# Final combine of a mixture-of-experts block: idle TensorE products ahead of the weighted sums, and one gather moved up Pool's list

## What is computed

```python
e_w, e_idx = lax.top_k(e_prob, MOE_TOP_K)            # two experts per token
w = g_w * e_w / sum(e_w)
out = einsum('tef,efd->td', silu(gate) * up * combine, w_down)   # = w0*y0 + w1*y1 per token
x = x + g2 * rms_norm(out, post_norm_ffn[l])
```

## Time and profile before

| what | us |
|---|---|
| median of 3 runs | 970.72 |
| lowest and highest run | 970.71, 973.47 |
| the profiled execution, its own time | 972.9 |
| its span, first to last instruction | 971.1 |

### The profile page before, as it was taken

One profiled execution on the slowest core, in us unless ns is written; L12 is line 12 of the kernel. 1 busy time (PEld: TensorE's weight loads), 2 busy tenths in 40 slices (PEclk: granted clock), 3 DMA queues, 4 the chain that ended last, 5 costly groups with the idle time before them and its releaser, 6 DMA issues.

```text
span 971.1 us, 15126 instructions
## 1 busy us (share of the span) xinstructions
PE 923.7 (95%) x5341; PEld 544.2 (56%) x5341; DVE 518.7 (53%) x959; ACT 318.5 (33%) x649; POOL 232.9 (24%) x282
## 2 busy tenths in 40 slices
PE   8999999999989999998999999989999999999953
PEld 6544444444546666667656665575555555555521
DVE  3375447444765666666588885663333333333347
ACT  3230002212545434432233332243333333333333
POOL 2200001122700670002354422012222222222125
PEclk9999999999999999999999999999999999999977
DMA  9996425000490000006023327978999999999694
GB/s 340 385 329 230 181 100 142 0 1 0 171 410 32 2 1 1 2 1 241 23 87 117 101 87 309 411 243 318 401 423 374 423 412 404 416 418 411 243 355 194
DMA packets 61618, 212.07 MB, mean 218 GB/s; under 512 B 17103, under 2 KB 28503, under 8 KB 46050
## 3 DMA queue, kind: packets, MB, share of 16 engines
q1 hardware_dynamic: 52820, 193.12, 51.9%
q0 software_dynamic: 7424, 17.85, 4.9%
q10 hardware_dynamic: 1296, 0.07, 0.1%
HBM read 179.85 MB, written 39.94 MB: 226 GB/s over the span
## 4 chain that ended last, share of the span: by engine, by line
PE 46%; DMA 3%; DVE 2%; issue 2%; ACT 1%; POOL 1%; POOLq 0%; ACTq 0%; DVEq 0%; SPq 0%
PE PS L1883 16%; PE PS L1732 11%; PE PS L1909 8%; PE PS L1857 2%; DMA y_g<-y_all 1%; PE PS L1694 1%; PE PS L1892 1%; PE PS L1710 1%; PE PS L1744 1%; PE PS L1756 1%; DMA x_g<-y_all,late_ext 1%; PE PS L1939 1%; PE PS L1683 1%; PE PS L1675 1%; PE PS L1638 1%
## 5 line engine op out<-in xcount | busy, mean ns | idle before, releaser
L1883 PE MATMUL PS<-ring,xg_T 128*64 x736 | 162.7, 379 | 1.0 <-ACT xg_T L2058 1.0
L1883 PE MATMUL PS<-near_gu,xg_T 128*64 128x256 f32 x736 | 162.7, 379 | 0.0
L1883 PEld LDWEIGHTS PS<-ring,xg_T 128*64 128x64 f32 x736 | 100.7, 137 | 60.3 <-issue 13.7
L1732 PE MATMUL PS<-w_out_sb,cat_T 128*128 128x512 f32 x256 | 116.8, 597 | 0.4 <-ACT cat_T L1979 0.4
L1069 PE MATMUL PS<-hT,w_x 128*128 128x512 f32 x256 | 112.1, 594 | 0.0
L1883 PEld LDWEIGHTS PS<-near_gu,xg_T 128*64 128x64 f32 x736 | 100.7, 137 | 0.0
L486 POOL TENSOR_SCALAR rstd<-stat 128x1 f32<-128x1 f32 (+1 forms) x45 | 18.0, 400 | 287.1 <-ACT junk L675 175.6
L1909 PE MATMUL PS<-ring,hid_T 128*64 x184 | 83.8, 598 | 0.4 <-DVE hid_T L2509 0.4
L1909 PE MATMUL PS<-near_dn,hid_T 128*64 128x512 f32 x184 | 83.9, 598 | 0.0
L1069 PEld LDWEIGHTS PS<-hT,w_x 128*128 128x128 f32 x256 | 47.8, 190 | 58.5 <-issue 58.2
L2500 DVE TENSOR_TENSOR hid<-PS,hid_s 128x128 f32<-128x128 f32 x46 | 11.2, 287 | 127.4 <-PE PS L1883 127.4
(11 more groups left out here) (380 smaller groups left out, 1532.3 us busy)
## 6 DMA issues: line engine op xcount, KB each, us to landing
ring<-in_w_gate_dram SPq DMA_DIRECT2D x32, 1024.0 KB, 11.6
ring<-in_w_up_dram SPq DMA_DIRECT2D x32, 1024.0 KB, 13.7
ring<-in_w_down_dram SPq DMA_DIRECT2D x32, 1024.0 KB, 16.0
ada_later<-in_ada_w_dram SPq DMA_DIRECT2D x16, 1024.0 KB, 4.8
y_all<-zeros SPq DMA_DIRECT2D x1, 14336.0 KB, 38.5
ada_first<-in_ada_w_dram SPq DMA_DIRECT2D x16, 512.0 KB, 8.9
y_g<-y_all SPq DMA_DIRECT2D x8, 1024.0 KB, 15.7
x_in<-in_x_dram SPq DMA_DIRECT2D x8, 512.0 KB, 7.8
```

The lines of the kernel that those rows point to most:

```text
L1732: last = pe.matmul(BANK[sorted(out_banks(t))[j]], cat_T[t % 2][:, k, :], w_out_sb[:, k, j * HALF:(j + 1) * HALF], start=(k == 0), stop=(k ...
L1883: last = pe.matmul(BANK[2 + s_][rows_, 0:FF], xg_T[b][:, k, rows_], gu[u][:, s_, k, :], start=(k == 0), stop=(k == KC - 1))
```

## The change

Pool issues the ninth tile's second gather, with the two waits in front of it, right after the root of tile 1 instead of after the addition of tile 1's residual. TensorE gets 26 idle products between the branch at the end of its steps and its first weighted tile. The loads of `y_g` stay as they are.

```diff
@@ Pool, final combine @@
                 root(0)
                 root(1)
+                scattered(STEPS)
+                pool.wait_ge(S["other_here0"], 16)
+                other_rows(1)
                 pool.wait_ge(S["x2_back"], 16 * NT)
                 root(2)
                 residual(1)
-                scattered(STEPS)
-                pool.wait_ge(S["other_here0"], 16)
-                other_rows(1)
                 root(3)
                 root(4)
                 residual(3)
@@ TensorE, after its steps @@
                 steps(pe, run)
 
+                busy(7, 26)
                 for n, t in enumerate(PE_TILES):
                     pe.wait_ge(S["w_diag"], n + 1)
                     pe.wait_ge(S[f"yg_loaded{t}"], 16)
```

## The result

The change takes 977.25 us (median of 5 runs, 976.73 to 978.42) against 970.88 for the kernel before (5 runs, 970.71 to 973.47). The ratio is 1.0065, with a 95% interval of 1.0054 to 1.0077: slower by 6.4 us, where 0.5 was forecast and 973.7 was the upper end. The profiled execution took 978.42 us with a span of 976.0, against 972.9 and 971.1 before.

The account below looks back on a forecast made before the run. The final combine's start of `summed(LAST)` was taken as the bound, the gather arriving last; DVE ready at 953.7 + 1.15 + 0.3 = 955.15 against 954.62 gives +0.5, so 970.7 + 0.5 = 971.2 us, range 969.5 to 973.7.

Parts of the forecast that it names:

- the two blocks of queue 8: TensorE's code fetched after its branch, at 929.05 and 929.25, taken to land at about 930.4 and 931.4.
- the clock that has just fallen: TensorE's clock drops to 1.2 GHz at about 930.3, just before the idle products start at 930.4.
- the low start of the idle products: On TensorE, the first 23 idle instructions run at the low clock, out by 935.2, at 0.21 us each.
- the late products: Rival: TensorE's idle products start at 931.4 with a late clock, tile 1 ends 1.5 us late; +1.8 us, 972.5; chance 0.14.
- when the idle products start: On TensorE behind the branch: forecast 930.4, bounds 928.2 (no stall) and 931.4.
- the prediction's worst case: Latest bound for ACT's square of tile 1: 1.5 us later, with start at 931.4 and clock back 5.6 us after.
- the prediction's own sum: DVE ready for `summed(LAST)` at 953.7 + 1.15 (root 2) + 0.3 (tile 1) = 955.15, against 954.62: +0.5 us.
- which cover tile 1 has: TensorE waited for tile 1's rows until 935.6 anyway, so the code fetch after the branch was free before.
- The 52 instructions: The 26 idle products on TensorE: from 930.4, 23 out by 935.2, the other 29 take 3.3 us, done at 938.5.
- the 13.9 of its sister: Rival: Pool's moved gather takes 13.9 us like the first gather, landing 958.4 to 958.5; 974.6 us; chance 0.08.
- Its price in front of root 2: Issuing the gather on Pool before the root of tile 2 makes that root start 1.15 us late, 945.47 instead of 944.32.
- The rival of the held clock: Rival: no stall at TensorE's branch, so the clock holds and tile 1 runs warm; 1.0 us faster, 969.7; chance 0.2.

Follow-up runs that it names:

- e2_pool_only: The kernel before with Pool's gather move alone, no idle products: 971.26 us against 970.64, ratio 1.0000.
- e5_straight_idle: The kernel before with TensorE's branch turned round and 26 idle products in the usual way, Pool as before: 969.61 us against 971.36, ratio 0.9982.
- e6_straight: The kernel before with TensorE's branch turned round so the usual way falls through, no idle products: 969.84 us against 971.36, ratio 0.9980.
- e7_straight_both: The whole change (26 idle products and Pool's move) with TensorE's branch turned round: 968.45 us against 971.36 for the kernel before, ratio 0.9973.
- e9_straight14_both: The kernel before with the branch turned round, 14 idle products and Pool's move: 968.76 us against 971.05, ratio 0.9979.
- e10_straight_pool: The kernel before with the branch turned round and Pool's move, no idle products: 970.64 us against 971.05, ratio 0.9991.
- e8_straight_idle14: The kernel before with the branch turned round and 14 idle products, without Pool's move: 968.88 us against 971.36, ratio 0.9968.
- e4_idle_double: The kernel before with 52 idle products behind the jump, Pool as before: 980.41 us against 970.64, ratio 1.0098.

## Why the prediction was wrong

**The place was right, two sizes were not.** It named the jump, the two blocks of queue 8, the clock that has just fallen, the low start of the idle products. It had this as its forecast with +0.5 us, and the late products as a rival with +1.8.

*First, when the idle products start.* This is the step that failed. I took the landing of the first block, worked out from the share of one packet, as the end of the stall: 2.2 us after the last product, 3.2 at most. It is 4.5 to 5.0 us in all five kernels that have idle products behind the jump. The first of the two blocks starts on its queue 0.3 to 0.8 us after the last product, and TensorE's first instruction comes 4.1 to 4.3 us after that start, in these five and in `e2_pool_only`, whether the packet of that block took 0.95 us or 1.84. The packets showed that code was fetched; their duration was not the duration of the stall. What the sequencer does in the rest of that time no row shows. The trace of before held only an upper bound: TensorE was idle for 7.54 us, so a stall of any length up to that was covered and possible. The bounds should have run from 0 to 7.5 us, not to 3.2. (Even with them the prediction's worst case was small: 27 slow instructions from 931.4 and 25 fast ones put tile 1 1.8 us late, not 1.5.)

This one step accounts for the two profiled executions. The square of tile 1 starts 16.4 us after the last product instead of 13.6, so 2.8 us late where 0.3 was taken. In the prediction's own sum DVE is then ready at 953.7 + 1.15 + 2.8 = 957.65, which is 3.0 us after the 954.62 of before; measured, with the drift taken out, it is 2.8 (29.2 against 26.4).

*Second, which cover tile 1 has.* I read from one execution that its rows land 7.4 us after the last product and took that as a property of the kernel. In `e2_pool_only` they land after 2.4, and tile 1's start is set by the stall itself, 4.5 us. From there the sum is another: 52 instructions at 8.0 us, less the 2.5 that a warm tile 1 saves (3.6 us for 6.1, `e5_straight_idle` and `e6_straight`), gives 5.5 us. `summed(LAST)` is 5.4 to 5.5 us later in the two runs of the change than in `e2_pool_only`, and the medians are 4.9 to 6.0 apart. Which of the two bounds holds in the median execution of the kernel before was not traced: in the seven traces with the jump the rows land after 2.4, 4.0, 6.1, 6.1, 6.4, 7.4 and 7.4 us. The spans speak for the stall. From the start of `summed(LAST)` to the end it is 16.4 to 16.5 us in all 13 traces, and the last expert product ends at 928.5 us on average. The median spans of the kernel before on the three chips, 968.8 to 969.5 us, then put its `summed(LAST)` some 24 to 24.6 us after that product (an estimate), nearer to the 23.7 of `e2_pool_only` than to the 26.4 that I had read. That the profiled execution was itself 2 us above the median stood in my first paragraph, and I did not ask what was slow in it.

A last piece stays open. The time of an execution outside its span is 1.7 to 1.9 us in the kernel before, but 2.3 to 2.5 at the median in the three runs with 26 products behind the jump, and not in the one with 52. That is 0.5 to 0.7 us of the loss, and no run says why.

*What held.* The 52 instructions take 7.96 us, 8.1 by my sum. Tile 3 follows tile 1 directly. The gather took 6.6 us at its new place (5.8 to 9.0 in the other five kernels that have the move), not the 13.9 of its sister, so that rival fell. Its price in front of root 2, 1.15 us, was measured at 1.1, and 1.0 of it reaches the end of the changed kernel, as the sum had it. Its gain appears only when TensorE is early, as `e7_straight_both` against `e5_straight_idle` shows. The Trainium skill (DMA: Bandwidth & Descriptors, Queues, rings and completion order) says that the engines take turns between their queues; these landings fit that better than the sister's row did, but no run here shows the turns.

*The rule that I used only in part.* The Trainium skill (Runtime: NRT & Kernel Launch, Instruction fetch mechanics) says that a taken branch beyond the fetched blocks stalls the engine. The runs agree: 4.5 to 5.0 us with the jump, none without it. I used it for the moment at which the idle products start, and not for what it meant for the kernel before: that its TensorE already stood still there.

The rival of the held clock had the right gain for another program. With the branch turned, the whole change is 2.6 us under the kernel before by its ratio (0.9973), where the rival gave 1.0.

## What to carry to other kernels

TensorE stood still for 4.5 to 5.0 us behind a jump over a second copy of its loop, and a wait for data could hide it; before putting work behind such a jump, try the branch turned round, so that the usual way falls through. How the stall depends on the length of the code that is jumped over was not measured. ACT and DVE pass the same branch with no gap (in the rows of `e2_pool_only` each starts its first instruction of the combine before its last one of the steps has ended), so a jump alone does not make a stall. They have far fewer instructions (959 on DVE in the whole kernel, 5393 on TensorE) and had been idle just before; which of the two spared them was not tested. A step in front of a chain of waits is paid for only when that chain is the one that ends last: Pool's move left the median alone by itself, cost 1.0 us behind the late idle products, and gained 1.1 in the traces with the branch turned. A wait of the profile with a releaser that was done long before (here the first diagonals, 3.5 us earlier) is a wait for something the trace does not name. And the slack that a late transfer gives should be read from several executions, above all when the one profiled is slower than the median.

## What the runs showed that I had not expected

The stall is nearly the same in every execution, 4.48 to 4.97 us in the five kernels with idle products behind the jump, while the landing of tile 1's rows, which had looked like the bound, moves between 2.4 and 7.4 us after the last expert product. And a TensorE that stays warm by products that read and write nothing of use can gain 1.9 us between medians (`e9_straight14_both` against `e10_straight_pool`) when they start without a gap. Without Pool's move it is less, 1.0 us with 14 of them and 0.2 with 26 (`e8_straight_idle14` and `e5_straight_idle` against `e6_straight`), both within the noise. Behind the jump the clock had fallen before they came, or fell as they came (`e4_idle_double`: 0.95 in the slice from 932 to 933, in which they start).
